# Eight instead of six tile pairs of the upward FFN by seven products, two in turn

## The reference

```
def conv_ffn(h, w_up, conv_w, w_down):       # h 512x1024, w_up 1024x5632
    gu = causal_dwconv(h @ w_up, conv_w)     # three taps along the tokens
    g, u = jnp.split(gu, 2, axis=-1)         # 2816 gate, 2816 up columns
    return (jax.nn.silu(g) * u) @ w_down
```

## Time and profile before

| | us |
|---|---|
| median of 3 runs | 1215.49 (1215.43 to 1216.43) |
| the profiled execution | 1215.4 |
| its span in the profile | 1213.6 |
| TensorE busy | 1199.9 |
| VectorE busy | 734.6 |
| GpSimd busy | 724.6 |
| ScalarE busy | 639.5 |

### The profile page before, as it was taken

One profiled execution on the slowest core, in us unless ns is written; L12 is line 12 of the kernel. 1 busy time (PEld: TensorE's weight loads), 2 busy tenths in 40 slices (PEclk: granted clock), 3 DMA queues, 4 the chain that ended last, 5 costly groups with the idle time before them and its releaser, 6 DMA issues.

```text
span 1213.6 us, 19024 instructions
## 1 busy us (share of the span) xinstructions
PE 1199.9 (99%) x6883; PEld 995.6 (82%) x6883; DVE 734.6 (61%) x1321; ACT 639.5 (53%) x1236; POOL 724.6 (60%) x558
## 2 busy tenths in 40 slices
PE   8999999999999999999999999999999999999997
PEld 7987777777788899987897777878898988898886
DVE  6555426757646777645597546446677765966224
ACT  6355545676645344455644666456555654333543
POOL 7674232353359776856384557548676775886842
PEclk9999999999999999999999999999999999999999
DMA  7332222122223333353142123323243343334332
GB/s 240 104 92 79 70 62 61 53 61 80 70 62 96 96 96 99 107 186 110 53 121 62 37 75 98 97 77 95 72 122 88 106 121 83 92 96 118 109 88 70
DMA packets 62437, 112.27 MB, mean 93 GB/s; under 512 B 6856, under 2 KB 11464, under 8 KB 62344
## 3 DMA queue, kind: packets, MB, share of 16 engines
q1 hardware_dynamic: 62200, 111.06, 31.8%
q10 hardware_dynamic: 144, 0.00, 0.0%
HBM read 108.87 MB, written 2.16 MB: 91 GB/s over the span
## 4 chain that ended last, share of the span: by engine, by line
PE 95%; DVE 3%; ACT 1%; issue 1%; POOL 1%; DMA 0%; SPq 0%; DVEq 0%; POOLq 0%; ACTq 0%
PE pb L1163 21%; PE pb L1164 21%; PE pb L1166 21%; PE pb L1225 5%; PE pb L1227 5%; PE pb L1226 5%; PE pb L1381 2%; PE pb L1357 2%; PE pb L1234 2%; PE pb L1324 1%; PE pb L1295 1%; PE pb L1297 1%; PE pb L1296 1%; PE pb L1278 1%; PE pb L1276 1%; PE pb L1346 1%
## 5 line engine op out<-in xcount | busy, mean ns | idle before, releaser
L2853 POOL TENSOR_TENSOR wlo<-raw,whi 128x512 fp32r<-128x512 f32 (+3 forms) x378 | 510.4, 1368 | 324.6 <-ACT whi L1588 323.4
L1163 PE MATMUL pb<-HH,whi 128*128 128x512 f32 x760 | 308.1, 405 | 0.0
L1164 PE MATMUL pb<-HL,whi 128*128 128x512 f32 x760 | 300.9, 396 | 0.0
L1166 PE MATMUL pb<-HH,wlo 128*128 128x512 f32 x760 | 300.0, 395 | 0.0
L1588 ACT ACTIVATE whi<-raw 128x512 fp32r<-128x512 f32 (+3 forms) x378 | 223.7, 614 | 108.2 <-PE pb L1166 56.5
L1163 PEld LDWEIGHTS pb<-HH,whi 128*128 128x128 f32 x760 | 143.5, 189 | 37.4 <-issue 4.6
L1164 PEld LDWEIGHTS pb<-HL,whi 128*128 128x128 f32 x760 | 143.2, 188 | 33.4 <-issue 2.9
L1166 PEld LDWEIGHTS pb<-HH,wlo 128*128 128x128 f32 x760 | 143.0, 188 | 33.1
L1724 ACT ACTIVATE P<-P,stat 128x256 f32<-128x256 f32 (+3 forms) x96 | 50.6, 527 | 78.0 <-DVE stat L2410 56.3
L2091 DVE SCALAR_TENSOR_TENSOR cv<-pb,vecs,cv 128x511 f32<-128x511 f32 x88 | 65.6, 745 | 5.4 <-ACT cv L1988 3.8
L2079 DVE TENSOR_TENSOR pb<-pb,rff 128x512 f32<-128x512 f32 x44 | 30.0, 695 | 40.7 <-PE pb L1166 34.0
(11 more groups left out here) (488 smaller groups left out, 2793.7 us busy)
## 6 DMA issues: line engine op xcount, KB each, us to landing
raw<-in_wall SPq DMA_DIRECT2D x368, 256.0 KB, 2.8
raw<-in_wall SPq DMA_DIRECT2D x8, 260.0 KB, 3.0
X<-in_xT SPq DMA_DIRECT2D x8, 256.0 KB, 6.1
X<-in_xT SPq DMA_DIRECT2D x2, 1024.0 KB, 7.5
outT<-PP SPq DMA_DIRECT2D x8, 256.0 KB, 2.5
raw<-in_wall SPq DMA_DIRECT2D x10, 192.0 KB, 2.4
raw<-in_wall SPq DMA_DIRECT2D x9, 128.0 KB, 2.4
cst<-in_cst SPq DMA_DIRECT2D x1, 832.0 KB, 8.0
```

The costliest lines, as they stand in the source:

```text
L1163: pe.do.matmul(b, hi, xh[k], start=start, stop=False, skip_group_check=tile[0] == "down")
L1164: pe.do.matmul(b, hi, xl[k], start=False, stop=False, skip_group_check=tile[0] == "down")
L1166: m = pe.do.matmul(b, lo, xh[k], start=False, stop=stop, skip_group_check=tile[0] == "down")
L2853: g.do.tensor_tensor(lo, x, hi.bitcast(F32), ALU.subtract).then_inc(*up(name, point))
```

## The change

UPS lists the seven-product pairs. Before they alternate with plain pairs from 6 to 16; now two stand in turn, with one plain pair behind each two (8, 11, 14). The numbers of the later groups (NUP and the down pairs') follow from the length of UPS. In `pair`, product(j-1), where j is the pair before the current one, is left out if that pair was itself one of UPS, since it then has been put already.

```
-UPS = (6, 8, 10, 12, 14, 16)
+UPS = (6, 7, 9, 10, 12, 13, 15, 16)
...
                 self.add("scaled", 1, j)
                 self.add("taps", 0, j)
                 self.add("swish", j)
-                self.add("product", j - 1)
+                if j not in UPS:
+                    self.add("product", j - 1)
```

## The result

The changed kernel takes 1263.58 us (median of 4, 1261.21 to 1266.27) against 1215.46: a ratio of 1.0395, 95% interval 1.0383 to 1.0408. It is slower by 48.1 us, where 36.2 were forecast; the direction and the main mechanism were right, the size was not, and the time lies above the range of 1242 to 1259. The profiled execution took 1261.21 us, with a span of 1259.4, so 45.8 us more span than before.

The account below looks back on a forecast made before the run. TensorE was taken to bound the kernel, busy 1199.9 of 1213.6 us. Shorter matmul work plus four pairs of stalls gave +29.6 us, clock falls 6.6 more: 1215.4 + 36.2 = 1251.6 us, range 1242 to 1259.

Parts of the forecast that it names:

- What is taken away: TensorE, pairs 6 to 16: two plain pairs become seven-product ones, 2.70 us less; 0.76 us of old waits also goes.
- The first stall: Second pair of each group: A11 waits for VectorE's product(5) to free its bank in pair 7, 6.22 us.
- The second stall: Plain pair behind each two: plain pair 8 waits for product(6) to free bank pb3, 2.04 us.
- Behind it VectorE ... catches up. So each group begins afresh: During each plain pair's 11.16 us VectorE has few sums and recovers, so all four groups show the same pattern.
- The rest of the kernel keeps its lengths: Outside the changed pairs and their waits, everything was expected to take as long as before.
- With four such falls: 4 x 1.66 = 6.6 us: TensorE's clock drops to 1.2 GHz in each 6.2 us wait, losing 1.66 us after restart; 2.0 us waits cause none.
- the stalls without the clock: Rival: TensorE waits add 29.6 us but its clock never falls, 1245.0 us; chance 0.2.
- only throughput counts: Rival: VectorE's work fits, so the waits vanish and the kernel is faster, 1211.9 us; chance 0.04.
- half a walk: Rival: S1 and S2 do not delay product(5), so the first wait is 3.38 us; 1233.6 us, chance 0.07.
- more than the walk: Rival: clock falls last twice as long, or GpSimd's 1 us of spare fails in each group; 1258.3 us, chance 0.12.
- the higher of the two sums: Whole kernel: the total including clock falls, +36.2 us, rather than the total at full clock, +29.6 us.

Follow-up runs that it names:

- both-edits run: Changed kernel with the plain pair's gate tile in a bank without a gate tile and 24 spare matmuls in each long stall: 1237.22 us.
- sums-late run: Changed kernel with VectorE making S1 and S2 of each second pair behind product(j) of the tile before the first one, not in front: 1253.47 us.
- the long stalls were filled: Changed kernel with 24 spare 128x512 matmuls in each of the four long stalls: 1257.26 us.
- downward bank exchanged: Changed kernel with banks 0 and 7 exchanged in the fixed bank list of the downward products: 1258.77 us.
- one-place run: Changed kernel with six seven-product pairs at 6, 7, 9, 11, 13, 15, so two stand in turn at one place: 1227.46 us.
- the plain pair's bank alone: Changed kernel, but the gate tile of a plain pair behind two seven-product ones takes no bank holding a gate tile: 1245.82 us.

## Why the prediction was wrong, and where it was right

Two steps of the prediction failed. The larger is the statement that the rest of the kernel keeps its lengths; the other is the size of the clock's term.

- **What is taken away**, 2.70 + 0.76 us: near. The both-edits run shows 3.1 us, and the account with 3.46 meets the spans of three kernels within 1.3 us.
- **The first stall**, 6.22: measured 6.30, 5.94, 6.28, 5.93 as idle time, 6.46 to 6.09 from start to start. Right in size, place and cause, and in its two parts (the sums-late run).
- **The second stall**, 2.04: measured 1.98, 1.90, 1.98, 1.98. Right, and only a matter of banks.
- **"Behind it VectorE ... catches up. So each group begins afresh"**: right; the four groups have nearly the same stalls.
- **"The rest of the kernel keeps its lengths"**: wrong, and the larger of the two errors. The prediction followed the planner's banks from pair 6 to plain pair 17 and stopped. The downward part takes its first bank from a fixed list, and the changed plan leaves the last gate tile in it. The stall is 5.25 us, and 2.8 of low clock in the profiled execution: 8.0 us. Taking it away alone gave 4.8 in the median (1258.77 us, just inside the range), adding it to the kernel before 7.3.
- **"With four such falls: 4 x 1.66 = 6.6 us"**: the mechanism was right and the term too small. In the profiled execution the four falls at the long stalls lost 6.4 us (12.9 us of low running), as the term has it; a fifth fall, behind a short stall, lost 1.7 more. Such a fall was ruled out ("one of 2.0 less"), and that was wrong: one short stall in four had one here, four in four once the long stalls were filled. In the same groups with the downward bank exchanged 14.4 us were lost, by longer falls and by two falls behind short stalls. That the four long falls met the term so closely is partly luck.
- Sum of both in the profiled execution: 36.2 - 33.0 + 32.3 (the eight stalls as measured) + 8.0 + 1.5 = 45.0, of the 45.8 measured. The median lies 2.4 us above the profiled execution, and the mean clock of its slower runs is 0.981 where that of the profiled one is 0.983.
- The rivals "the stalls without the clock", "only throughput counts" and "half a walk" fell. Of "more than the walk", the clock did cost more than the sum had, mainly by falls that the sum did not count; the wait for GpSimd did not appear in the changed kernel.

By the rule of the Trainium skill (TensorE: Matmul & The Clock Gate, Part 1) that idling takes the speed away and work gives it back, the higher of the two sums was the one to take; the windows of 0.50 behind the stalls agree, and with the stalls filled or gone (the both-edits run) the clock stayed at 1.00.

## What to carry to other kernels

When a planner hands out banks by age, a change in one stage shifts them for everything behind, and a part with banks written out by hand is where the two meet: follow the last holder of each bank to the end of the program, not only through the stage that was changed. An in-order queue can hold up a faster neighbour though its busy share is far below one (VectorE 16.4 of 21.1 us here): walk the queue from the last instruction whose time is known to the one that frees the buffer. Price a TensorE stall above its length: here 37.5 us of stalls cost 48.4 in the profiled execution, and stalls of two microseconds could bring a fall of the clock too.

## What the runs showed of the hardware

The granted clock fell to 1.2 GHz behind some stalls of 2.0 us and not behind others: one of four in the changed kernel, two of four in the same groups with the downward bank exchanged, four of four with the long stalls filled. In that last run it fell 1.2 us after TensorE had started again behind the first of them (884.30 to 885.54). In the long stalls it fell after 2.4 us (changed kernel, 866.26 to about 868.6), 3.6 us (the one-place run), 1.9 us (downward bank exchanged, 910.15 to about 912.1) or 4.8 us (the plain pair's bank alone, 984.04 to 988.89). How long TensorE then ran slowly differed for one and the same program part: in the four groups, 16.3 us at half speed in one execution and 28.8 in another with the same stalls. What decides between them is not settled by these runs.

The time of a kernel with such stalls spreads accordingly: 5.1 us over four runs of the change, 8.9 us with the sums late, where the fastest run (1247.55 us) had a mean granted clock of 0.993 and the slowest (1256.48) one of 0.982, and 0.7 us where spare matmuls and another bank kept the clock up.
